# Two rms norms' factors applied behind the products that read them, the residual stream transposed half by half beside the other half's products, and the last product summed tile by tile

## The reference

```
y  = rmsnorm(h, norm_mix_g) @ w_in           # attention of 8 heads, and a convolution
h  = h + concat([att, conv]) @ w_out
xq = rmsnorm(h, norm_x_g) @ w_xq             # 4 heads of 256, against 256 memory rows
pr = softmax(xq . xk * 256 ** -0.5)
h  = h + (pr . xv) @ w_xo
u  = rmsnorm(h, norm_mlp_g) @ w_up           # 1024 -> 4096
h  = h + square(relu(u)) @ w_down            # 4096 -> 1024
return rmsnorm(h, norm_final_g)
rmsnorm(x, g) = x * rsqrt(mean(x * x) + 1e-6) * g
```

## Time and profile before

| | |
|---|---|
| median of 3 runs | 1748.59 us (1746.74 to 1750.09) |
| the profiled execution's own time | 1745.93 us |
| its span, first to last instruction | 1744.1 us |
| mean granted TensorE clock | 0.974 of full speed |
| TensorE busy | 1602.2 us (92%) |
| VectorE, ScalarE, GpSimd busy | 762.7, 622.1, 621.0 us |

### The profile page before, as it was taken

The page is one execution under the profiler, slowest core; times in us unless marked ns, Lnnn a source line. Parts: engine busy times, 40 slices in busy tenths (PEclk is TensorE's granted clock), DMA queues, the critical chain, the costliest instruction groups (busy, mean ns, idle before and its releaser), DMA issues.

```text
span 1744.1 us, 18478 instructions
## 1 busy us (share of the span) xinstructions
PE 1602.2 (92%) x7476; PEld 1295.9 (74%) x7476; DVE 762.7 (44%) x1355; ACT 622.1 (36%) x886; POOL 621.0 (36%) x266
## 2 busy tenths in 40 slices
PE   1899999999698999999998998998989899999996
PEld 1688867778587887788876886776856688888885
DVE  7899224556565352233238794743222321012113
ACT  3443553432225332133315224562432443123310
POOL 0552332233244444444435542013313244444441
PEclk9999999999899999999998998999999999999998
DMA  9393432259224353323324331002201233233331
GB/s 304 92 147 103 115 92 66 85 182 311 99 85 145 97 171 113 103 77 98 104 85 126 122 97 49 1 13 85 73 25 61 74 97 107 88 94 97 97 97 61
DMA packets 221029, 180.26 MB, mean 103 GB/s; under 512 B 24072, under 2 KB 184200, under 8 KB 220816
## 3 DMA queue, kind: packets, MB, share of 16 engines
q1 hardware_dynamic: 211728, 166.48, 33.0%
q10 hardware_dynamic: 9216, 12.60, 2.2%
HBM read 172.49 MB, written 6.55 MB: 103 GB/s over the span
## 4 chain that ended last, share of the span: by engine, by line
PE 77%; DVE 15%; ACT 4%; issue 2%; POOL 1%; DMA 1%; ACTq 0%; DVEq 0%; SPq 0%
PE bank L601 14%; PE bank L602 14%; PE bank L603 14%; PE bank L623 7%; PE bank L624 7%; PE bank L625 7%; DVE bank L1990 5%; PE bank L661 3%; PE bank L1002 1%; PE bank L919 1%; DVE grow L1588 1%; PE bank L949 1%; PE bank L831 1%; ACT scr L1068 1%; ACT att_area L1396 1%
## 5 line engine op out<-in xcount | busy, mean ns | idle before, releaser
L2131 POOL TENSOR_TENSOR w_lo<-raw,w_hi 128x1024 fp32r<-128x1024 f32 (+1 forms) x248 | 602.8, 2434 | 1030.6 <-ACT w_hi L1042 1030.6
L601 PE MATMUL bank<-h_hi,w_hi 128*128 128x512 f32 x1032 | 406.5, 394 | 5.6 <-DVE h_lo L1495 2.6
L603 PE MATMUL bank<-h_hi,w_lo 128*128 128x512 f32 x1032 | 402.6, 390 | 0.0
L602 PE MATMUL bank<-h_lo,w_hi 128*128 128x512 f32 x1032 | 402.4, 390 | 0.0
L1042 ACT ACTIVATE w_hi<-raw 128x1024 fp32r<-128x1024 f32 (+1 forms) x248 | 260.0, 1050 | 392.0 <-PE bank L625 312.8
L601 PEld LDWEIGHTS bank<-h_hi,w_hi 128*128 128x128 f32 x1032 | 194.1, 188 | 52.0 <-DVE h_lo L1495 5.5
L603 PEld LDWEIGHTS bank<-h_hi,w_lo 128*128 128x128 f32 x1032 | 194.0, 188 | 40.6
L602 PEld LDWEIGHTS bank<-h_lo,w_hi 128*128 128x128 f32 x1032 | 194.1, 188 | 40.4 <-issue 1.0
L1562 DVE TENSOR_TENSOR x_tok<-x_tok,bank 128x512 f32<-128x512 f32 x32 | 21.9, 684 | 225.5 <-PE bank L625 225.5
L625 PE MATMUL bank<-w_hi,u_lo 128*128 128x512 f32 x256 | 101.3, 396 | 0.0
L624 PE MATMUL bank<-w_lo,u_hi 128*128 128x512 f32 x256 | 101.2, 395 | 0.0
(11 more groups left out here) (380 smaller groups left out, 2472.8 us busy)
## 6 DMA issues: line engine op xcount, KB each, us to landing
raw<-in_w_in SPq DMA_DIRECT2D x57, 512.0 KB, 4.0
raw<-in_w_ffn_up SPq DMA_DIRECT2D x44, 512.0 KB, 3.8
raw<-in_w_up SPq DMA_DIRECT2D x32, 512.0 KB, 4.0
raw<-in_w_down SPq DMA_DIRECT2D x32, 512.0 KB, 3.7
ada_ring<-in_w_ada SPq DMA_DIRECT2D x24, 512.0 KB, 5.6
raw<-in_w_ffn_down SPq DMA_DIRECT2D x20, 512.0 KB, 3.6
raw<-in_w_s_glu SPq DMA_DIRECT2D x16, 256.0 KB, 3.2
raw<-in_w_mlstm_down SPq DMA_DIRECT2D x8, 512.0 KB, 6.6
```

What stands on the lines that cost most here:

```text
L601: te.matmul(ps, wv[0][:, i, :], rh, start=(i == 0), stop=False)
L602: te.matmul(ps, wv[0][:, i, :], rl, start=False, stop=False)
L603: last = te.matmul(ps, wv[1][:, i, :], rh, start=False, stop=(i == kt - 1))
L2131: gp_.tensor_tensor(W_LO[s_][:, 0:n], raw[:, RAW_SLOT[key], 0:n], W_HI[s_][:, 0:n].bitcast(F32), ALU.subtract).then_inc(*lo_made.up(key))
```

## The change

1. Behind out and xo, the sums in x_tok are transposed as they are, without the factor. The first column half's features (0 to 3) are transposed after the second block of the second half's products (`turn_sums`), the other four behind the first half of the next product: `feature_pair` makes the first two blocks of xq (or u) over features 0 to 3, then over 4 to 7. The statistics are taken behind the low parts.
2. The factor of the query norm goes into the scale of the exponential and into its shift (x_plus, x_minus); that of the u norm goes squared (inv2) onto the sums of ud0 and ud1 (`add_scaled`), as relu and square keep a positive factor.
3. The transposed stream for xq lies in new buffers x_hi and x_lo; xn4 and xn5 are gone.
4. out goes over its features in the order 4, 6, 0, 2, and the last attention output is transposed after its first block.
5. Cross-attention has four buffers of probabilities and two of transposed ones, may use all eight banks, and its steps stand in another order.
6. ud1 goes through `tail`: the last two feature pairs of both column halves are made tile by tile, with two more weight slots (tail_u). The final norm's sums of squares come from ScalarE (`squares`), and norms and stores are made tile by tile, the stores in halves of 512 columns.

The core of the diff (TensorE's list, then ScalarE's, VectorE's and SyncE's):

```diff
+        tail_u = place("tail_u", X + 18432, [4, BW], F32R)
...
+        x_hi = place("x_hi", X + 6144, [KD, S], F32R)
+        x_lo = place("x_lo", X + 10240, [KD, S], F32R)
         xqT = place("xqT", X + 2048, [KD, S])
-        xps_t = place("xps", X + 6144, [2, TT, NMEM])
-        xps = [xps_t[:, i] for i in range(2)]
-        xpT = place("xpT", X + 8192, [MT, S])
+        xps_t = place("xps", X + 17408, [XH, TT, NMEM])
+        xps = [xps_t[:, h] for h in range(XH)]
+        xpT_t = place("xpT", X + 21504, [2, MT, S])
+        xpT = [xpT_t[:, i] for i in range(2)]
...
+        squares = place("squares", X + 22528, [2 * TT, S])
...
+        def token_blocks(stage, w, r0, ncols, kt, order=None):
+            ROWS[stage] = list(order or range(0, kt, 2))
             for c in range(ncols // 512):
-                for g in range(0, kt, 2):
+                for g in ROWS[stage]:
...
+        token_blocks("out", io["w_out_2"][0], 0, D, KD, (4, 6, 0, 2))
...
+            if half_ == 0:
+                token_blocks("ud0", io["w_down_2"][0], 0, D, UH)
+        UD_HEAD, UD_TAIL = [(c, g) for c in range(2) for g in range(0, UH - 4, 2)], [(c, g) for c in range(2) for g in (UH - 4, UH - 2)]
+        for c, g in UD_HEAD + UD_TAIL:
+            BLOCKS["ud1", c, g] = [w_rows(io["w_down_2"][0], UH * P, c, g, 2)]
...
+        SLOT = {("mix", 1, 4): 3, ("mix", 1, 6): 4, ("fd1", 1, FH - 1): 5, ("fd1", 1, 8): 6, ("ud1", 1, UH - 4): 7, ("ud1", 1, UH - 2): 8}
...
+        def product(key, ps, wv, kt, hi, lo, ready, i0=0, i1=None):
+            for i in range(i0, i1 or kt):
                 rh, rl = at(hi, lo, i)
                 pe.wait_ge(*ready[i])
                 te.matmul(ps, wv[0][:, i, :], rh, start=(i == 0), stop=False)
                 te.matmul(ps, wv[0][:, i, :], rl, start=False, stop=False)
                 last = te.matmul(ps, wv[1][:, i, :], rh, start=False, stop=(i == kt - 1))
-            last.then_inc(*gemm.up(key))
+            if i1 is None:
+                last.then_inc(*gemm.up(key))
...
+        def feature_pair(keys, hi, lo, ready, frees, between):
+            made = []
+            for key, free in zip(keys, frees):
+                ps = take("acc", key, free)
+                (wv,) = block(key)
+                product(key, ps[:, :], wv, KD, hi, lo, ready, 0, KD // 2)
+                made.append((key, ps, wv))
+                if key == keys[0]:
+                    between()
+            for key, ps, wv in made:
+                product(key, ps[:, :], wv, KD, hi, lo, ready, KD // 2)
...
+            ring["misc"], turn["misc"] = [4, 5, 6], 2
             cat_ready = [o_ls[i] for i in range(AT)] + [cn_ls[i] for i in range(AT)]
+            def turn_sums(stage, f, taken, free):
+                for f_ in range(f, f + 4):
+                    pe.wait_ge(*taken[f_ // 4, TT - 1])
+                    transpose((stage, f_), [x_tok[:, t, f_ * P:(f_ + 1) * P] for t in range(TT)], free[f_])
...
+                for g in ROWS["out"]:
                     token(("out", c, g), KD, h_hi, h_lo, cat_ready, lambda c, t: out_r[c, t])
-            pe.wait_ge(*xn_set["w3"])
-            for f in range(KD):
-                transpose(("h4", f), [xn4[:, t, f * P:(f + 1) * P] for t in range(TT)], h4_lo[f])
-            freed[7] = taps_done[AT - 1]
-            ring["misc"] = [4, 5, 6, 7]
-            turn["misc"] = 3
+                    if (c, g) == (0, 0):
+                        turn_output(AT - 1)
+                        freed[7] = taps_done[AT - 1]
+                        ring["misc"], turn["misc"] = [4, 5, 6, 7], 3
+                    if (c, g) == (1, 6):
+                        turn_sums("h4", 0, out_r, h4_lo)
...
+            turn["acc"] = 3
             h4_ready = [h4_lo[i] for i in range(KD)]
-            def x_query(m):
-                feature(("xq", m), h_hi, h_lo, h4_ready, xq_out[m])
+            feature_pair([("xq", 0), ("xq", 1)], x_hi, x_lo, h4_ready, [xq_out[0], xq_out[1]], lambda: turn_sums("h4", 4, out_r, h4_lo))
...
+            x_queries(2)
+            x_scores(0)
+            x_queries(4)
+            x_scores(1)
+            x_queries(6)
+            ring["misc"], turn["misc"] = list(range(8)), 7
+            x_scores(2)
+            x_turn(0)
+            x_scores(3)
+            x_turn(1)
+            x_values(0)
+            x_turn(2)
+            x_values(1)
+            x_turn(3)
+            x_values(2)
+            x_values(3)
+            ring["misc"], turn["misc"] = [4, 5, 6, 7], 3
             for c in range(2):
-                for g in range(0, KD, 2):
+                for g in ROWS["xo"]:
                     token(("xo", c, g), KD, xo_hi, xo_lo, [xo_ls[i] for i in range(KD)], lambda c, t: xo_r[c, t])
-            pe.wait_ge(*xn_set["c3"])
-            for f in range(KD):
-                transpose(("h5", f), [xn5[:, t, f * P:(f + 1) * P] for t in range(TT)], h5_lo[f])
+                    if (c, g) == (1, 2):
+                        turn_sums("h5", 0, xo_r, h5_lo)
...
+                u_ready = [u_ls[k_ * UH + i] for i in range(UH)]
+                if k_ == 0:
+                    feature_pair([("u", 0), ("u", 1)], h_hi, h_lo, h5_ready, [u_r[0], u_r[1]], lambda: turn_sums("h5", 4, xo_r, h5_lo))
+                for m in range(max(2, k_ * UH), (k_ + 1) * UH):
                     feature(("u", m), h_hi, h_lo, h5_ready, u_r[m])
-                for c in range(2):
-                    for g in range(0, UH, 2):
-                        token((f"ud{k_}", c, g), UH, u_hi, u_lo, [u_ls[k_ * UH + i] for i in range(UH)], lambda c, t: ud_r[k_][c, t])
+                if k_ == 0:
+                    for c in range(2):
+                        for g in ROWS["ud0"]:
+                            token(("ud0", c, g), UH, u_hi, u_lo, u_ready, lambda c, t: ud0_r[c, t])
+            for c, g in UD_HEAD:
+                token(("ud1", c, g), UH, u_hi, u_lo, u_ready, None, range(4 * c, 4 * c + 4))
+            tail("ud1", UH, [[(g, ("ud1", c, g), 0) for c, g in UD_TAIL if c == c_] for c_ in range(2)], u_hi, u_lo, u_ready, lambda c, t: ud1_r[c, t])
...
+                for g in ROWS["out"]:
                     high_ahead("out", c, g)
-            norm_tiles("w0", xn4, 0, ["w0", "w1"])
-            norm_tiles("w1", xn4, 2, ["w2", "w3"])
-            for f in range(KD):
-                turn_plain("h4", f, h_hi[:, f, :], col("g_x", f), h4_hi)
-            def x_query(m):
-                high_ahead("xq", m)
-                act.wait_ge(*gemm["xq", m])
-                act.wait_ge(*turned["h4", KD - 1])
-                sc.activation(xqT[:, m, :], ps_of(("xq", m))[:, :], ACT.Copy).then_inc(*xq_out.up(m))
+                    if (c, g) == (0, 0):
+                        turn_plain("o", AT - 1, h_hi[:, AT - 1, :], 1.0, o_hs)
+                    if (c, g) == (1, 6):
+                        for f in range(4):
+                            turn_plain("h4", f, x_hi[:, f, :], col("g_x", f), h4_hi)
+            for f in range(4, KD):
+                turn_plain("h4", f, x_hi[:, f, :], col("g_x", f), h4_hi)
+            act_root("w", TT, 0, 4)
...
+                act.wait_ge(*x_scaled.all)
...
+                    sc.activation(xps[h][:, t, :], ps_of(("xs", h, t))[:, 0:NMEM], ACT.Exp, bias=x_mx[h][:, t:t + 1], scale=x_plus[:, t:t + 1], accum_out=x_den[h][:, t:t + 1]).then_inc(*x_p.up((h, t)))
...
+            x_queries(0)
+            x_queries(2)
+            x_exps(0)
+            x_queries(4)
+            x_exps(1)
+            x_queries(6)
+            x_exps(2)
+            x_turn(0)
+            x_exps(3)
+            x_turn(1)
+            x_values(0)
+            x_turn(2)
+            x_values(1)
+            x_turn(3)
+            x_values(2)
+            x_values(3)
...
+                    if (c, g) == (1, 2):
+                        for f in range(4):
+                            turn_plain("h5", f, h_hi[:, f, :], col("g_mlp", f), h5_hi)
...
-            act.wait_ge(*turned["h5", KD - 1])
+            act_root("c", TT, 0, 4)
...
+            high_to(len(ORDER))
+            for t in range(TT):
                 for c in range(2):
-                    for g in range(0, UH, 2):
-                        high_ahead(f"ud{k_}", c, g)
-            act_root("z0", 2, 0, 4)
-            act_root("z1", 2, 2, 4)
+                    act.wait_ge(*ud1_r[c, t])
+                    sc.activation(squares[:, 2 * t + c, :], x_tok[:, t, c * 512:(c + 1) * 512], ACT.Square, accum_out=sm[:, c, t:t + 1]).then_inc(*sq_sum.up((c, t)))
+                if t > 0:
+                    act_root(f"z{t - 1}", 2 if t == 1 else 1, 0 if t == 1 else t, 4)
...
+        def add_scaled(stage, c, t, b, taken):
+            x = x_tok[:, t, c * 512:(c + 1) * 512]
+            dve.wait_ge(*tile_done[stage, c, t])
+            ve.scalar_tensor_tensor(x, bank[b][:, :], inv2[:, t:t + 1], x, ALU.mult, ALU.add).then_inc(*taken.up((c, t)))
+        def sums(stage, parts_, hi, lo, gain, taken):
+            for c in range(2):
```

(55 more changed lines are left out.)

166 lines of the change are left out of this document (67 added, 99 removed).

## The result

The changed kernel takes 1708.68 us (median of 4 runs, 1706.48 to 1710.45) against 1748.96 us (4 runs, 1746.74 to 1750.09): a ratio of 0.9775, 95% interval 0.9763 to 0.9786, or 40.3 us less. The forecast was 1710 us, 38.5 us less. Its profiled execution took 1708.97 us, with a span of 1707.2 us and a mean granted clock of 0.981.

A forecast was written before the change was run, and what follows sets the result against it. TensorE's products and its standstills were taken to bound the kernel. Terms 0.5 + 7.7 + 17.4 + 8.0 + 5.5 = 39.1, less deductions 38.5, gave 1707.4 from the profiled 1745.9, so a median of 1710 us; range 1704 to 1722.

The forecast's parts named there:

- A: Last head's transposes after one block of output products: the 0.59 us wait behind VectorE's scaling is filled, gain 0.5 us.
- B: Seam from out to xq: norm factor deferred off the path, new 1.3 us wait at third weight block, net gain 7.7 us.
- C: Cross-attention reordered with more buffers: all eight waits go, value groups and following products speed up, gain 17.4 us.
- If the clock does not hold, 11.9 is the floor: Cross-attention: without the full clock, the reordering would still gain at least 11.9 us.
- D: Seam from xo to u, same pattern with h_hi staying low: new wait of 1.7 us, gain 8.0 us.
- E: The end, tiles finishing one by one: 8.0 us behind the last product instead of 13.2, gain 5.2, plus 0.3.
- The clock sags in the attention: Rival for cross-attention: the clock drops anyway on thin work and transposes there double, giving 1717 us; chance 0.15.
- Transposes don't count: Rival for the four seam transpose batches: transposes are not work for the clock, so time is lost, 1724 us; chance 0.06.
- GpSimd holds up the norm chain: Rival at both seams: a split beside VectorE's small norm operations delays the third weight block by 4.7 us, 1719; chance 0.05.
- The third block is not late: Rival at the seams: ScalarE gets to the third weight block's split in time, giving 1707 us; chance 0.09.
- Slower: Rival: after the new wait at xq 2 TensorE stays at 1.2 GHz, ending above 1760 us; chance 0.03.
- the 0.6 deducted for changes of kind: Term of the sum: 0.1 us off for each of six changes between kinds of TensorE instruction.

The follow-up runs named there:

- e1_turn_first: The changed kernel with the last head's transposes behind the first out block (0,4) instead of the third (0,0): first stretch 63.26 us against 65.01, ratio 0.9768 to the kernel before.
- e4_old_attention: The changed kernel with cross-attention's order and buffers as before, norm factors still deferred: 22.3 us slower than the changed kernel, ratio 0.9908 to the kernel before.
- e3_no_tail: The changed kernel with the last down-projection and final norm as in the kernel before: 6.3 us slower than the changed kernel, ratio 0.9807 to the kernel before.

## Why the prediction was right

**A was wrong.** "Products over features 4 and 5 come first" is so, but the transposes don't stand behind them (the text on the change has this wrong too, in its point 4): they stand behind block (0, 0), the third. I put down a gain of 0.5 us. As built the step lost 1.0: it took away the wait of 0.59 and brought one of 1.50. In the place I had read it would have gained 0.75, for e1_turn_first is 1.75 us better. The step that failed is reading the condition without the order of the loop around it.

**B** was right in mechanism. With t = 0 at the end of the last output product (1218.35), I had the first query product at -0.2, the root done near 10.6 and the third block at 14.1; they came at -0.2, 10.2 and 13.7 (1232.01), with a wait of 0.71 in place of 1.3. By the sum of the prediction, with the measured times, that is a gain of 24.71 - 13.66 - 1.8 = 9.25 us against 8.7. Without A's slip the stretch is 63.26 us, 10.0 less than before, against 9.2 forecast.

**C** was low by 1.4 us: 17.8 instead of 16.4, the high x_hi included. All eight waits went (11.9 us). The value groups gave 5.1 us, counted to the next instruction's start (18.4 to 13.3), for 5.0. The transposes I had left out: eight take 0.88 us from their start to the next instruction's (1289.01 to 1289.89), where the kernel before had 1.09 busy and then a wait, so 0.85 us in four groups; the ends of the scores in front of a wait gave 0.7 in the same way. One term of the sum was misread. I had put the 0.79 us of the first product behind a value group down to the clock, and took 0.5 us for it. That product takes 0.79 in the changed kernel as well (1296.35), with no low clock before it, and in e4_old_attention behind the first group, at 1.00. It belongs to the change from the values to a split product, and only 0.2 us went, with one such place of two. So the terms are 11.9 + 5.1 + 0.85 + 0.7 + 0.2, less 1.0 for the high x_hi: 17.8. "If the clock does not hold, 11.9 is the floor" was never tested by the change: the clock held.

**D** was right: pair done, then 1.25 us of waiting (1.7 forecast), 8.4 gained (8.0 forecast).

**E** gave 5.9 at the end against 5.2. Square and read of the sum took 0.72 until the next operation could start (1701.06 to 1701.78) and 0.85 had been set; VectorE was free when the last tile came (add at 0.43 us, not 0.6), and the store took 2.4 us (1704.81 to 1707.2), not 3.05. The two scalings ended at 4.96 us, forecast 5.0, so nearly the whole difference is the store. The 0.3 for the high weights came as 0.1; e3_no_tail, which compares like with like, has 0.24.

**The rivals.** *The clock sags in the attention*: no, 1.00 throughout. *Transposes don't count*: nothing of it shows; 16 in a row leave the clock at 1.00, and the next products run at full pace. (The row of before that I had read as 16 between two products was 12, a wait of 0.48 us, and 4.) The Trainium skill (TensorE: Matmul & The Clock Gate, Part 4) has it that they don't count as busy in the same way; the trace does not show it as far as 16 in a row between products. The page speaks of a transpose mode of the engine, and no run here shows whether these transposes use it. *GpSimd holds up the norm chain*: the mechanism is there, only behind the chain. In VectorE's timeline, and then GpSimd's:

```profile
1229.39 0.16 DVE L1606 TENSOR_TENSOR sm<-sm 128x4 f32<-128x4 f32 x1
1229.59 2.40 DVE L2165 TENSOR_SCALAR sm<-sm 128x4 f32<-128x4 f32 x1
```
```profile
1229.58 4.75 POOL L2250 TENSOR_TENSOR w_lo<-raw,w_hi 128x1024 fp32r<-128x1024 f32 x2 [13.02 <-ACT w_hi L1105]
```

An operation on four numbers a partition, of a size that took 0.16 us just before it, lasted as long as one split beside it. It makes the factor of the exponentials' shift (x_minus), which is wanted much later, so it cost nothing. The Trainium skill (SBUF — State Buffer, "Who interferes with whom") says that a tensor_scalar can run in a mode that takes the port pair shared with GpSimd, and that the engine that issues first then holds the pair for its whole instruction. The trace agrees: the split had started 0.01 us before. *The third block is not late*: it was, by 0.71 and 1.25 us. *Slower*: no low clock followed those waits.

Summed by the stretches, the first gave 1.0 us less than forecast, the attention 1.4 more, D 0.4 and E 0.5 more, and the 0.6 deducted for changes of kind is not to be found on top of them: 40.4 for 38.5. That the two lie within 2 us is in part luck. By the steps, A was 1.5 us too high, and B, C, D and E were 0.5, 1.4, 0.4 and 0.5 too low; with A in its right place the miss would have been 3.7 us.

## What to carry to other kernels

Before pricing a seam, write down the order in which every queue reaches it: what decided the last microseconds here was an instruction's place in a list (transposes one block before their reader, a root ahead of a split), not its length. Price a wait on TensorE with its clock, and not by the row of one execution: the same 12 us of waits, with all that came with them, cost some 19 us in one kernel here and 22 in another, and no run shows what decides between them. When an interleaving brings little, look for what is late next before taking it out.

## What was not expected of the hardware

- The pace of a 128 x 512 product depends on where its two operands lie: 0.2267 us with both in the low or both in the high part of the memory, 0.2333 otherwise; over the two down-projections 4.8 us.
- The half clock is not a fixed price of a pattern: with the same order and the same waits the second head's group of values was granted 0.66 in the kernel before (1293.00 to 1298.00) and 0.55 in e4_old_attention, and the first head's 0.65 (1269.40 to 1274.30) and 1.00.
- The part ahead of the change varied by 5.4 us (last head's values at 1163.16 to 1168.60) between executions, while the stretches behind repeated to 0.1 us.
